# Taking and tapping a block's first chunk at its own signal, and one swap moved to the next stage in a transformer kernel

## The reference, cut to what matters

```python
def compress(k, pe, w1, w2):
    blk = k[cmp_idx] + pe[None, :, None, :]          # windows of 32 positions, step 16
    blk = blk.transpose(0, 2, 1, 3).reshape(n_cmp, G, CMP_BLOCK * dh)
    return jax.nn.silu(blk @ w1) @ w2

def conv_ffn(h, w_up, conv_w, conv_b, w_down):       # h: 512 x 1024, w_up: 1024 x 5632
    u = h @ w_up
    up = jnp.pad(u, ((0, 0), (CONV_WIDTH - 1, 0), (0, 0)))
    y = conv_b
    for j in range(CONV_WIDTH):
        y = y + conv_w[j] * up[:, j:j + S]
    gate, val = jnp.split(y, 2, axis=-1)
    return (jax.nn.gelu(gate, approximate=True) * val) @ w_down
```

## Time and profile before

| | |
|---|---|
| median of 3 runs | 2127.97 us |
| profiled execution, its own time | 2125.32 us |
| its span (first to last instruction) | 2123.5 us |
| TensorE busy | 2061.2 us, 97% |
| VectorE busy | 1217.8 us, 57% |
| ScalarE busy | 793.1 us, 37% |
| bytes moved by DMA | 188.52 MB, mean 89 GB/s |

### The profile page before, as it was taken

The page is one execution under the profiler, slowest core; times in us unless marked ns, Lnnn a source line. Parts: engine busy times, 40 slices in busy tenths (PEclk is TensorE's granted clock), DMA queues, the critical chain, the costliest instruction groups (busy, mean ns, idle before and its releaser), DMA issues.

```text
span 2123.5 us, 25577 instructions
## 1 busy us (share of the span) xinstructions
PE 2061.2 (97%) x9944; PEld 1668.9 (79%) x9944; DVE 1217.8 (57%) x1717; ACT 793.1 (37%) x1231; POOL 24.4 (1%) x45
## 2 busy tenths in 40 slices
PE   8999999999999999999999999999999999999997
PEld 6766778888888888777788888878786678888886
DVE  5678635454435355555675574663537757647475
ACT  4248242332212232345343342442427734324242
POOL 1000000000000000000000000000000000000000
PEclk9999999999999999999999999999999999999998
DMA  5410412322222222321122223122220022222221
GB/s 188 141 59 2 142 47 99 109 100 99 96 88 95 99 99 90 109 90 60 60 99 99 99 79 114 70 94 90 99 90 31 21 79 80 99 99 99 99 84 55
DMA packets 34320, 188.52 MB, mean 89 GB/s; under 512 B 4392, under 2 KB 8648, under 8 KB 14608
## 3 DMA queue, kind: packets, MB, share of 16 engines
q1 hardware_dynamic: 32448, 181.24, 24.2%
q0 software_dynamic: 1568, 5.65, 1.1%
q10 hardware_dynamic: 208, 0.33, 0.0%
HBM read 182.54 MB, written 2.11 MB: 87 GB/s over the span
## 4 chain that ended last, share of the span: by engine, by line
PE 88%; DVE 4%; PEld 3%; ACT 2%; issue 2%; DMA 1%; DVEq 1%; PEldq 0%; ACTq 0%; SPq 0%
PE bank L411 23%; PE bank L413 22%; PE bank L412 22%; PE bank L492 3%; PE bank L497 3%; PE bank L493 3%; PE bank L1212 2%; PE bank L1242 2%; PE bank L1229 2%; DVE w_lo L359 1%; PE bank L653 1%; PEld bank L411 1%; PEld bank L413 1%; PEld bank L412 1%; PE bank L2250 1%
## 5 line engine op out<-in xcount | busy, mean ns | idle before, releaser
L345 ACT ACTIVATE w_hi<-w_raw 128x2048 fp32r<-128x2048 f32 (+3 forms) x174 | 314.4, 1807 | 810.7 <-PE bank L413 687.8
L411 PE MATMUL bank<-a_hi,w_hi 128*128 128x512 f32 x1376 | 540.0, 392 | 4.8 <-DVE w_lo L359 1.8
L413 PE MATMUL bank<-a_hi,w_lo 128*128 128x512 f32 x1376 | 535.6, 389 | 0.0
L412 PE MATMUL bank<-a_lo,w_hi 128*128 128x512 f32 x1376 | 535.6, 389 | 0.0
L359 DVE TENSOR_TENSOR w_lo<-w_raw,w_hi 128x2048 fp32r<-128x2048 f32 (+3 forms) x174 | 374.9, 2157 | 143.1 <-ACT w_hi L345 142.9
L411 PEld LDWEIGHTS bank<-a_hi,w_hi 128*128 128x128 f32 x1376 | 258.4, 188 | 61.2 <-issue 3.7
L413 PEld LDWEIGHTS bank<-a_hi,w_lo 128*128 128x128 f32 x1376 | 258.3, 188 | 54.4
L412 PEld LDWEIGHTS bank<-a_lo,w_hi 128*128 128x128 f32 x1376 | 258.5, 188 | 53.2 <-issue 0.5
L411 PE MATMUL bank<-big_halves,w_hi 128*128 128x512 f32 x616 | 240.6, 391 | 3.2 <-DVE w_lo L359 3.0
L413 PE MATMUL bank<-big_halves,w_lo 128*128 128x512 f32 x616 | 239.7, 389 | 0.0
L412 PE MATMUL bank<-big_halves,w_hi 128*128 128x512 f32 x616 | 239.7, 389 | 0.0
(11 more groups left out here) (340 smaller groups left out, 2421.5 us busy)
## 6 DMA issues: line engine op xcount, KB each, us to landing
w_raw<-in_w_fu SPq DMA_DIRECT2D x44, 1024.0 KB, 4.8
w_raw<-in_w_up SPq DMA_DIRECT2D x16, 1024.0 KB, 4.8
w_raw<-in_w_down SPq DMA_DIRECT2D x16, 1024.0 KB, 4.8
w_raw<-in_w_fd SPq DMA_DIRECT2D x16, 1024.0 KB, 4.8
w_raw<-in_w_fd SPq DMA_DIRECT2D x8, 768.0 KB, 4.2
w_raw<-in_w_rqk SPq DMA_DIRECT2D x4, 1024.0 KB, 5.2
w_raw<-in_w_rvg SPq DMA_DIRECT2D x4, 1024.0 KB, 4.9
w_raw<-in_w_gate SPq DMA_DIRECT2D x4, 1024.0 KB, 5.0
```

The lines of the kernel that those rows point to most:

```text
L345: act.activation(w_hi[slot][:, cols], raw[slot][:, cols], ACT.Copy).then_inc(hi_half_ready.sem if half == 0 else hi_ready.sem, 1)
L411: pe.matmul(out, w[0], x[0], start=first, stop=False)
L412: pe.matmul(out, w[0], x[1], start=False, stop=False)
L413: return pe.matmul(out, w[1], x[0], start=False, stop=last)
```

## The change

Two things. In the FFN's blocks up, each chunk has a signal of its own when it has been scaled out of PSUM (`first_out`, then `evacuated`). In second blocks (odd numbers) VectorE takes the first chunk at `halves_done`, and ScalarE makes its first tap *ahead of* the split of the weights of block b + 2; in the others both wait as before for the whole block, and ScalarE's tap needs only the first chunk's signal. VectorE's two taps now go chunk by chunk, with a drain in each. In the compression, `halves_swapped` stands behind the first position tile of `vg`, no longer inside `kcvc`.

```diff
-                                between={(0, 8): positions_turned, (1, 12): halves_swapped}))
+                                between={(0, 8): positions_turned}))
...
-                                     late_act=lambda act, b, slot, m: hidden_act(act) if b == 0 else None, between={(0, TT - 1): hidden}))
+                                     late_act=lambda act, b, slot, m: hidden_act(act) if b == 0 else None, between={(0, 0): halves_swapped, (0, TT - 1): hidden}))
...
-                    def late_act(act, b, slot, m, tap=tap):
+                    def second(slot, m):
+
+                        return (slot - m["slot"]) % 2 == 1
+
+                    def first_tap(act, b, slot, m, tap=tap):
+                        act.wait_ge(first_out.sem, m["first"] + b + 1)
+                        act.wait_ge(hid_ready.sem, m["hid"] + 2 * b - 2)
+                        act.activation(z[slot][:, 0, :], u[slot][:, 0, 2:S + 2], ACT.Identity, scale=tap(2, b, 0),
+                                       bias=tap(3, b, 0)).then_inc(tapped.sem, 1)
+
+                    def early_act(act, b, slot, m, first_tap=first_tap):
+                        if second(slot, m):
+                            first_tap(act, b, slot, m)
+
+                    def late_act(act, b, slot, m, tap=tap, first_tap=first_tap):
+                        if not second(slot, m):
+                            first_tap(act, b, slot, m)
                         act.wait_ge(evacuated.sem, m["evac"] + b + 1)
-                        act.wait_ge(hid_ready.sem, m["hid"] + 2 * b - 2)
-                        for c in range(2):
-                            act.activation(z[slot][:, c, :], u[slot][:, c, 2:S + 2], ACT.Identity, scale=tap(2, b, c),
-                                           bias=tap(3, b, c)).then_inc(tapped.sem, 1)
+                        act.activation(z[slot][:, 1, :], u[slot][:, 1, 2:S + 2], ACT.Identity, scale=tap(2, b, 1),
+                                       bias=tap(3, b, 1)).then_inc(tapped.sem, 1)
...
                     def early_dve(dve, b, slot, m):
-                        dve.wait_ge(products_done.sem, m["prod"] + b + 1)
 
                         dve.wait_ge(tapped.sem, m["tap"] + 2 * b - 2)
-                        for c in range(2):
-                            ins = dve.tensor_tensor(u[slot][:, c, 2:S + 2], bank[2 * slot + c][:, :], inv[:, :], ALU.mult)
-                        ins.then_inc(evacuated.sem, 1)
+                        if second(slot, m):
+                            dve.wait_ge(halves_done.sem, m["half"] + ((b + 1) // 2 if isinstance(b, int) else m["i"] + 1))
+                        else:
+                            dve.wait_ge(products_done.sem, m["prod"] + b + 1)
+                        dve.tensor_tensor(u[slot][:, 0, 2:S + 2], bank[2 * slot][:, :], inv[:, :], ALU.mult).then_inc(first_out.sem, 1)
+                        if second(slot, m):
+                            dve.wait_ge(products_done.sem, m["prod"] + b + 1)
+                        dve.tensor_tensor(u[slot][:, 1, 2:S + 2], bank[2 * slot + 1][:, :], inv[:, :], ALU.mult).then_inc(evacuated.sem, 1)
 
-                    def late_dve(dve, b, slot, m, tap=tap):
-                        dve.wait_ge(evacuated.sem, m["evac"] + b + 1)
+                    def late_dve(dve, b, slot, m, tap=tap):
+                        dve.wait_ge(first_out.sem, m["first"] + b + 1)
                         for c in range(2):
+                            if c == 1:
+                                dve.wait_ge(evacuated.sem, m["evac"] + b + 1)
                             dve.wait_ge(tapped.sem, m["tap"] + 2 * b + c + 1)
                             dve.scalar_tensor_tensor(z[slot][:, c, :], u[slot][:, c, 1:S + 1], tap(1, b, c), z[slot][:, c, :], ALU.mult, ALU.add)
-                        dve.drain()
-                        for c in range(2):
+                            dve.drain()
                             dve.scalar_tensor_tensor(z[slot][:, c, :], u[slot][:, c, 0:S], tap(0, b, c), z[slot][:, c, :],
                                                      ALU.mult, ALU.add).then_inc(part_used.sem, 1)
...
-                    stages.append(dense(f"fu{l}{g}", two_chunks(a_tiles), early_dve, late_dve, none, late_act, **(begin if g == 0 else {})))
+                    stages.append(dense(f"fu{l}{g}", two_chunks(a_tiles), early_dve, late_dve, early_act, late_act, **(begin if g == 0 else {})))
```

More of the change, by code:

```diff
@@ L259, in build @@
         gelu_ready, tapped = tally("gelu_ready"), tally("tapped")
-        hid_ready = tally("hid_ready")
+        hid_ready, first_out = tally("hid_ready"), tally("first_out")
         inputs_in = [tally(f"inputs_in{i}") for i in range(4)]
@@ L365, in marks @@
                     "prod": products_done.n, "evac": evacuated.n, "rows": rows_done.n, "rowsout": rows_out.n,
-                    "part": part_ready.n, "pused": part_used.n, "gelu": gelu_ready.n, "tap": tapped.n, "hid": hid_ready.n,
+                    "part": part_ready.n, "pused": part_used.n, "gelu": gelu_ready.n, "tap": tapped.n, "hid": hid_ready.n, "first": first_out.n,
                     "sq": squared.n, "sum": summed.n, "mixed": mixed.n, "half": halves_done.n, "hout": half_out.n,
@@ L2610, in ffn @@
                     b_hid, b_part = hid_ready.n, part_ready.n
-                    stages.append(dense(f"fu{l}{g}", two_chunks(a_tiles), early_dve, late_dve, none, late_act, **(begin if g == 0 else {})))
+                    stages.append(dense(f"fu{l}{g}", two_chunks(a_tiles), early_dve, late_dve, early_act, late_act, **(begin if g == 0 else {})))
+                    first_out.n += n
                     part_used.n += 2 * n
```

## The result

| | before | with the change |
|---|---|---|
| median | 2129.1 us (5 runs, 2126.3 to 2131.34) | 2116.93 us (5 runs, 2115.03 to 2118.56) |
| traced execution, its own time | 2125.32 us | 2115.03 us |
| its span | 2123.5 us | 2113.2 us |
| mean granted clock of the traced execution | 0.990 | 0.993 |

What follows compares the result with a forecast made beforehand. The prediction took TensorE's single chain of products, busy 97% of the span, as the bound; -4.8 - 3.0 - 0.9 + 0.8 = -7.9 us from a base of 2127.97 gave 2120.1 us, range 2116 to 2125.

Steps and rivals of the forecast that it cites:

- The compression: Swap moved behind the first tile of `vg`: TensorE's queue gains 5.1 us, `hidden` waits 0.3, together -4.8 us.
- the wait of 0.3 for the values: In the compression, `hidden` wants the values' half at 68.4, VectorE has it at 68.7: 0.3 us lost.
- The lower bound of 2.9: Compression's smallest gain, -2.9 us: unprofiled clock not down at the swap (1.75 less), values as late again.
- The end of an FFN: Chain from an FFN's last block up into its product down: 1.5 us shorter, twice, -3.0 us.
- the ends of the groups of 8: Ends of groups of 8 FFN blocks: low half 0.23 us too late at four places, -0.9 us gained.
- The rule on the drain: VectorE's taps at FFN ends: the skill's rule makes a fourth drain free (-3.3 us); the forecast counted +0.14 for it.
- The start of an FFN: Block 3's weight rounding waits behind block 1's first tap; TensorE loses 0.4 us, twice, +0.8 us.
- one rival at one place: At the swap, most executions keep the clock through the 3.4 us pause: 1.75 less gain, 2121.9 us; chance 0.12.
- `hidden` gave back 0.45, not 2: Rival in the compression: the wait moves into `hidden`; 2 us late gives -5.9, 3.5 late -4.4, about 2123 us; chance 0.10.
- the low half was the whole wait: Rival at the FFN's end: something unmoved holds it, the 3.9 us fall away, -4.0, 2124 us; chance 0.06.
- ScalarE never blocked the stream: Rival in odd FFN blocks: ScalarE's rounding hangs on VectorE, stalling TensorE; slower, about 2132 us; chance 0.06.

Runs made afterwards that it cites:

- the variant with the late tap: The changed kernel with ScalarE's first tap always behind the split of the weights: 2118.33 us, ratio 0.9936 to the kernel before.
- the swap alone: The kernel before with only the swap of key halves moved into `vg`, the FFNs as before: 2122.62 us against 2131.33, ratio 0.9958.
- the scores cut: Both kernels with the compression's score products cut into four pieces with dense steps between: kernel before 2128.61 us, changed kernel 2118.18 us.

## Why the prediction was right

The forecast was 2120.1 us in 2116 to 2125; measured 2116.93. The direction and the mechanisms held, the size was 7.9 for 12.2 us. The measured time lies only 0.9 us above the lower end of the range, which was drawn from the bounds and the spread of the runs, without the norms, where the sum turned out too small; that it is inside is partly luck.

- **The compression, forecast -4.8: -4.8 in the trace.** `vg` near 57.7: 57.79. Swap near 59.3 without a wait: 59.33. `hidden` over by 75.9: 75.86. Two small errors cancel in the 4.8: TensorE's queue gained 5.3 up to `hidden` (71.04 to 65.75, forecast 5.1), and the wait of 0.3 for the values came as about 0.45. The rotation was not 0.9 us ahead of the swap but 0.4. The lower bound of 2.9 is a slip: by its own terms (1.75 less, and 0.3 once more for the values) it is 2.75.
- **The end of an FFN, -3.0, and the ends of the groups of 8, -0.9.** The wait for the low half went from 1.5 to 0.16 us, the chain from 9.80 to 8.23 (forecast 1.5 shorter, measured 1.57). The small losses of the earlier trace rows are gone, about 0.25 us each.
- **The rule on the drain.** Dependent taps stand 0.82 apart (the pair at 1369.46 and 1370.28 in the changed kernel's timeline), independent ones 0.67 (1370.28 and 1370.95), so a drain more costs 0.15. The Trainium skill ("VectorE: DVE Perf Modes", "The DRAIN you can't avoid") says that the next op waits for the pipe to empty in any case and that a semaphore costs nothing extra. The prediction read it as though one more drain were free as well; the trace went the way of the rows.
- **The start of an FFN, +0.8: +0.34 twice.** Tap, rounding and low half came in the order of the sum, and the variant with the late tap took the price away. VectorE caught up, and no later block waited.
- Together -8.2 in the trace for -7.9: every term within 0.3 us.
- **What the sum left out: the clock away from the swap.** The sum ran on one trace of each place, and the clock stood in it as one rival at one place ("if most executions keep the clock through the 3.4 us, the swap is worth 1.75 less"). That can happen (one of three traces of the kernel before kept it), but most don't: four of the five traces with the whole pause fell. And the clock falls at other places too, at a cost of up to 3.2 us behind the scores. My first trace was the fastest of all executions of that kernel in the study, and it was already under all three timed ones when I took it. Of the 25 timed beside the variants, 21 have a mean clock of 0.986 or 0.987 and take 2128.9 to 2133.9 us. The changed kernel's ten timed ones have 0.990 to 0.993, and its one further trace 0.988. At the same mean clock of 0.990 the kernel before took 2125.32 and 2125.70, the changed one 2118.56 and 2120.17: 6.1 us apart, near the sum less the clock's share at the swap (8.2 - 1.7). That agrees but proves little: the mean clock is given to 0.001, which is 4.2 us at the lower level, up to 2.1 us of time.
- **A part of the missing 4 us is the FFN part's, and I put it at nothing.** In the norm behind the first FFN the clock is down for 10.2 us in each of the six traces whose FFNs are as before (the swap alone among them), and for 6.8 us in each of the eight that have the FFN part, with or without the swap's move. That norm takes 0.8 us less in them on average. The norm at the end of the program is 0.9 us shorter in six of the eight (0.4 and nothing in the other two) and the same within 0.1 in the six. Against it, four of the eight have a short fall near 1605 us that none of the six has, 1.2 to 1.3 us each; the norm ahead of the second FFN gives 0.1. Together this is about 1.0 us on top of the 3.4 of the FFNs' own steps. With the compression at 5.0 (the mean of six traces without the pause against five with the whole of it) the traces put the change at about 9.4 us. Why work that comes 1.7 us earlier meets a shorter fall was not tested.
- **What stays open.** The other 3 us of the 12.2 (1 of the 10.4 with the scores cut): why the timed executions of the kernel before fell so much more often than the changed kernel's. Behind the scores the traces of the two sets lose the same on average (2.1 and 1.8 us). A pause that is at times 4.0 or 4.2 us and not 3.4 is part of it (two of five traces with the whole pause), with 0.7 to 0.8 us each.
- The other rivals: `hidden` gave back 0.45, not 2; the low half was the whole wait (0.16 of it is left); ScalarE never blocked the stream after block 3.

## What to carry to other kernels

When the bound engine runs one long chain, write down the start of the same instruction in both traces every few hundred us: the steps in that difference give each part of a change its price, and show where the two kernels differ although nothing was changed there. Don't call that luck before several traces of each were set side by side: one such step here (the norm behind the first FFN) was the change's in every trace. One trace is one draw of the clock: where an engine idles or runs small products for some us, read two or three traces before pricing the place. Before moving a step earlier in a queue, ask which of its uses needs it: the early tap cost 0.4 us per FFN where a split of weights stood behind it, and helped only where none did, so the old place served both.

## What the runs showed of the hardware

TensorE's granted clock fell to its lower level (1.2 of 2.4 GHz) in one execution and stayed up in another at the same place, after the same work. At the swap it fell after 3.35 us of idle time (0.54 from 58.5 to 62.0) and not after 3.48 us (1.00). In or right behind 3.8 us of 32-column matmuls without any idle time it fell in 6 of 11 traces (0.66 from 105 to 115 us in one, 1.00 in another), which cost 3.2 us in four of them and 1.6 in two. The Trainium skill ("TensorE: Matmul & The Clock Gate", Part 1) says that what watches TensorE's activity runs free of the kernel's start; these rows fit that. Cut into four pieces with dense products between them, the same small matmuls left the clock up in three of three traces. And a place can fall for longer or shorter with what happened some 25 us ahead of it: behind the first FFN 10.2 us at the lower level in six of six traces, 6.8 in eight of eight whose FFN ends 1.6 us sooner.
